# Two of four quarters of a transposed activation go through VectorE and a DRAM scratch instead of TensorE

## The reference

```python
def first_block(x, ...):
    n = rmsnorm(x, attn_norm)
    mix = four_mixers(n @ w_in)                # gated delta net, mLSTM, RG-LRU, RWKV
    x = x + mix @ w_out                        # blocks o0..o3
    n = rmsnorm(x, ffn_norm)                   # operand "x1"
    x = x + (silu(n @ w_gate) * (n @ w_up)) @ w_down   # blocks fg, fu, d
    return rmsnorm(x, final_norm)

def second_block(x, mem, ...):
    h = rms_norm(x, norm_in_g)                 # operand "x2"
    proj = h @ w_in_2                          # first block of it: va0
    ya, yb, ym = moba(...), dilated(...), memory_attention(...)
    merged = sum(sigmoid(gate_i) * (y_i @ w_proj_i))
    return rms_norm(x + merged @ w_out_2, norm_final_g)
```

## Time and profile before

| | |
|---|---|
| time, median of 3 runs | 2382.24 us (2382.02 to 2383.36) |
| time of the profiled execution | 2382.23 us |
| its span in the trace | 2380.4 us |
| PE busy | 2355.0 us, 99% |
| DVE busy | 1489.1 us, 63% |
| ACT busy | 1129.3 us, 47% |
| POOL busy | 257.7 us, 11% |
| DMA queue of SP (q1) | 53.7% of the 16 engines' span |
| DMA queue of GpSimd (q0) | 3.3% |
| mean granted TensorE clock | 0.998 of full speed |

### The profile page before, as it was taken

The page is one execution under the profiler, slowest core; times in us unless marked ns, Lnnn a source line. Parts: engine busy times, 40 slices in busy tenths (PEclk is TensorE's granted clock), DMA queues, the critical chain, the costliest instruction groups (busy, mean ns, idle before and its releaser), DMA issues.

```text
span 2380.4 us, 31332 instructions
## 1 busy us (share of the span) xinstructions
PE 2355.0 (99%) x12768; PEld 1956.3 (82%) x12768; DVE 1489.1 (63%) x1929; ACT 1129.3 (47%) x1423; POOL 257.7 (11%) x383
## 2 busy tenths in 40 slices
PE   9999999999999999999999999999999999999998
PEld 7777789988888888888888888888888888888887
DVE  6887757787755656555565666555556655555555
ACT  6635446564543444444444464445444455344444
POOL 0100011210011111110111142200003200000000
PEclk9999999999999999999999999999999999999999
DMA  9643355645666566655665576655446644555563
GB/s 299 197 142 111 123 175 193 210 165 203 204 202 200 197 198 202 202 192 190 203 203 194 183 241 222 217 172 177 160 153 227 212 142 161 193 195 194 191 233 141
DMA packets 255344, 453.46 MB, mean 190 GB/s; under 512 B 12257, under 2 KB 77409, under 8 KB 252897
## 3 DMA queue, kind: packets, MB, share of 16 engines
q1 hardware_dynamic: 241984, 423.65, 53.7%
q0 software_dynamic: 12640, 27.28, 3.3%
q10 hardware_dynamic: 576, 0.53, 0.1%
HBM read 430.97 MB, written 10.49 MB: 185 GB/s over the span
## 4 chain that ended last, share of the span: by engine, by line
PE 92%; DVE 4%; ACT 1%; issue 1%; DMA 0%; POOL 0%; SPq 0%; ACTq 0%; DVEq 0%; POOLq 0%
PE pp L683 25%; PE pp L685 25%; PE pp L684 25%; PE pp L712 7%; PE pp L713 3%; DVE ringL L2016 1%; PE ps L642 1%; PE ps L1295 1%; PE ps L1309 1%; PE ps L831 0%; DMA raw<-in_w_in 0%; ACT ringH L1383 0%; PE pp L718 0%; PE pp L719 0%; PE pp L720 0%
## 5 line engine op out<-in xcount | busy, mean ns | idle before, releaser
L2016 DVE TENSOR_TENSOR ringL<-raw,ringH 128x1024 fp32r<-128x1024 f32 x779 | 962.5, 1243 | 647.5 <-ACT ringH L1383 645.0
L1383 ACT CAST ringH<-raw 128x1024 fp32r<-128x1024 f32 x779 | 814.8, 1050 | 972.2 <-PE pp L685 864.0
L683 PE MATMUL pp<-ringH,nS 128*128 128x512 f32 x1376 | 543.1, 395 | 0.0
L685 PE MATMUL pp<-ringH,nS 128*128 128x512 f32 x1376 | 536.3, 390 | 0.0
L684 PE MATMUL pp<-ringL,nS 128*128 128x512 f32 x1376 | 535.8, 389 | 0.0
L712 PE MATMUL pp<-nS,ringH 128*128 128x512 f32 x992 | 362.8, 407 | 6.6 <-DVE ringL L2010 2.8
L685 PEld LDWEIGHTS pp<-ringH,nS 128*128 128x128 f32 x1376 | 258.3, 188 | 54.5
L683 PEld LDWEIGHTS pp<-ringH,nS 128*128 128x128 f32 x1376 | 258.4, 188 | 52.9 <-issue 0.4
L684 PEld LDWEIGHTS pp<-ringL,nS 128*128 128x128 f32 x1376 | 258.5, 188 | 51.5 <-issue 0.2
L713 PE MATMUL pp<-nS,ringL 128*128 128x256 f32 x992 | 279.1, 281 | 0.0
L683 PE MATMUL pp<-ringH,xS 128*128 128x512 f32 x704 | 277.8, 395 | 0.0
(11 more groups left out here) (406 smaller groups left out, 2002.0 us busy)
## 6 DMA issues: line engine op xcount, KB each, us to landing
raw<-in_w_in SPq DMA_DIRECT2D x189, 1024.0 KB, 5.1
raw<-in_ffn_w_gate SPq DMA_DIRECT2D x44, 1024.0 KB, 5.4
raw<-in_ffn_w_up SPq DMA_DIRECT2D x44, 1024.0 KB, 5.1
raw<-in_ffn_w_down SPq DMA_DIRECT2D x44, 1024.0 KB, 5.0
raw<-in_w_out SPq DMA_DIRECT2D x32, 1024.0 KB, 5.1
raw<-in_w_mem_kv SPq DMA_DIRECT2D x16, 1024.0 KB, 5.5
AR<-AR POOLq DMA_DIRECT2D x304, 32.0 KB, 4.7
raw<-in_w_proj_a SPq DMA_DIRECT2D x8, 1024.0 KB, 5.1
```

Of the source, the lines that this page charges most:

```text
L683: mm(o, XH[:, ts(j)], WH, first, False)
L685: t_of[0] = mm(o, XL[:, ts(j)], WH, False, last)
L1383: e.copy(ringH[:, h % NSPL, 0:nh * cols], raw[:, u % NRAW, h0 * cols:(h0 + nh) * cols]).then_inc(*hi.tick(h))
L2016: tt2(ringL[:, h % NSPL, o], raw[:, u % NRAW, h0 * cols:(h0 + nh) * cols], ringH[:, h % NSPL, o].bitcast(F32), SUB).then_inc(*lo.tick(h))
```

## The change

The second and third quarter (q = 1, 2) of x1 and x2 are no longer turned by TensorE.

* Behind the drain of `o1.0`, `o2.0`, `d10.1` and `d10.2`, DVE transposes the 32x32 blocks of the quarter into a buffer `across[q]` (two instructions of 128x512).
* GpSimd then runs `hop`: it writes the 512 KB buffer to a scratch in DRAM with one DMA, waits until that has landed, and issues four DMAs of 128 KB that read it back into the same buffer with the blocks crossed.
* ACT and DVE make the high and low parts from that buffer (`landed_split`), waiting on the DMAs' semaphore.
* `fg0` and `va0` take the rows of their weights in the order k = 0 to 3, 12 to 15, 4 to 7, 8 to 11. The stages stand in the order quarter 0, quarter 3, quarter 1 (behind s8 of `fg0` / `va0`), quarter 2 (behind s12). `stat1` and `stat2` come behind them.
* The squares of `XB` for x2 move from the split stage to the drain of the `d10` blocks.

```diff
-    for q in range(4):
-        L.upto(f"o{q}.0")
-        L.step(3)
+    for q in (0, 3):
+        L.upto(f"o{q}.0", 3)
         L.weave(L.stage(f"split1.{q}"), 1)
+    for n, q in enumerate((1, 2)):
+        L.upto("o3.0", 7 + 4 * n)
+        L.run(f"split1.{q}")
...
-    for q in range(4):
-        L.upto(f"d{NG - 1}.{q}")
-        L.step(3)
+    for q in (0, 3):
+        L.upto(f"d{NG - 1}.{q}", 3)
         L.weave(L.stage(f"split2.{q}"), 1)
+    for n, q in enumerate((1, 2)):
+        L.upto(f"d{NG - 1}.3", 7 + 4 * n)
+        L.run(f"split2.{q}")
...
+        def hop(e, name, to, of, apart):
+            d = hold[name]
+            e.dma_start(d.rearrange("p (t n) -> p t n", t=2), of).then_inc(s_out, 16)
+            e.wait_ge(s_out, 16 * (1 + over.index(name)))
+            for j in range(4):
+                piece = d.rearrange("(i p) (t j c) -> j p t i c", i=4, t=2, j=4)[j]
+                for t in (slice(0, 1), slice(1, 2)) if apart else (slice(0, 2),):
+                    e.dma_start(to[32 * j:32 * j + 32, t, :].rearrange("p t (i c) -> p t i c", i=4), piece[:, t]).then_inc(s_over[name], 16)
...
+            turns = (0, 12, 4, 8) if tag in ("fg0", "va0") else None
...
+                k0 = turns[u // 4] if turns else (u + first_k) % nk
...   ACT
+            def landed_split(name, dst, gain, q):
+                def go(L):
+                    for k in range(4 * q, 4 * q + 4):
+                        e.wait_ge(s_over[f"{name}.{q}"], 64)
+                        act(dst[:, k, 0, :]..., in_runs(across[q])[:, :, k % 4, :], ACT.Copy, scale=gain(k))
+                    if name == "x2":
+                        for b in range(2):
+                            e.wait_ge(*pool.at("xg", q, b))
+                            square(XG, q, b, ssg, junk, "x2g")
+                    yield
...   DVE, at the end of drain(B)
+                if q in across:
+                    own(drain_v)
+                    for tt in range(2):
+                        e.transpose(by_quarter(across[q], tt), in_quarters(XB[:, :, 512 * q:512 * q + 512], tt))
...   GpSimd, in unit(i)
+                if s.last and tag in ("o1.0", "o2.0", f"d{NG - 1}.1", f"d{NG - 1}.2"):
+                    e.wait_ge(*drain_v.at("turned", tag, 1))
+                    hop(e, f"x{1 if tag[0] == 'o' else 2}.{q}", across[q], across[q], False)
```

More of the change, by code:

```diff
@@ L419, in program @@
             "fn_v")}
+        over = ["x1.1", "x1.2", "x2.1", "x2.2"]
+        s_out = sem("s_out")
+        s_over = {n: sem(f"s_over_{n}") for n in over}
         hold = {}
@@ L423, in program @@
             hold[nm] = nc.dram_tensor(nm, [128, n], F32).ap()
+        for n in over:
+            hold[n] = nc.dram_tensor("hop_" + n.replace(".", "_"), [128, 1024], F32).ap()
         def alias(name, off, shape):
@@ L1454, in squares @@
                 what = kind[B.tag]
-                x, to, name = (XB, junk, "x1") if what == "o" else (XC, junk3, "x3")
+                x, to, name = (XB, junk, "x1") if what == "o" else (XB, junk, "x2") if what == "d" else (XC, junk3, "x3")
                 for b in range(2):
                     e.wait_ge(*drain_v.at(*(("b0",) if b == 0 else ()), B.tag))
-                    square(x, int(B.tag[1]), b, ss, to, name)
+                    square(x, int(B.tag[-1] if what == "d" else B.tag[1]), b, ss, to, name)
             def high_h(g):
@@ L1503, in unit @@
                         drain(B)
-                    if kind[B.tag] == "q" and B.tag != "q3" or kind[B.tag] == "o" and B.tag[-1] == "0":
+                    if kind[B.tag] == "q" and B.tag != "q3" or kind[B.tag] == "o" and B.tag[-1] == "0" or B.tag.startswith(f"d{NG - 1}."):
                         squares(B)
@@ L1983, in scalar @@
                 "stat1": stat1,
-                **{f"split1.{q}": split1(q) for q in range(4)}, "stat2": stat2, **{f"split2.{q}": split2(q) for q in range(4)},
+                **{f"split1.{q}": split1(q) for q in (0, 3)}, "stat2": stat2, **{f"split2.{q}": split2(q) for q in (0, 3)},
+                **{f"split1.{q}": landed_split("x1", xS, lambda k: pc("ffn_norm", k), q) for q in (1, 2)},
+                **{f"split2.{q}": landed_split("x2", nS, lambda k: gg[:, k:k + 1], q) for q in (1, 2)},
                 "attA": attA, "attM": attM, "attB": attB,
@@ L2064, in drain @@
                             finish(b)
+                q = int(tag[-1]) if tag.startswith(f"d{NG - 1}.") else int(tag[1]) if what == "o" and tag[-1] == "0" else None
+                if q in across:
+                    own(drain_v)
+                    for tt in range(2):
+                        e.transpose(by_quarter(across[q], tt), in_quarters(XB[:, :, 512 * q:512 * q + 512], tt)).then_inc(
+                            *drain_v.tick("turned", tag, tt))
                 if tag in h_crossed:
@@ L2846, in stat2, with landed_split, go @@
                 yield
+            def landed_split(name, dst, gain, q):
+                def go(L):
+                    for k in range(4 * q, 4 * q + 4):
+                        h_, l_ = (dst[:, k, n, :].rearrange("p (a c) -> p a c", c=32) for n in range(2))
+                        e.wait_ge(*sp_a.at(name, k))
+                        stt(out=l_, in0=in_runs(across[q])[:, :, k % 4, :], scalar=gain(k), in1=h_.bitcast(F32), op0=MUL,
+                            op1=SUB).then_inc(*sp_v.tick(name, k))
+                    yield
+                return go
             def scaled_split(name, dst, pname, ks):
@@ L2943, in vector @@
                 **{f"mix{m}": split("mix", nS, lambda k: mix[:, k, :], range(4 * m, 4 * m + 4)) for m in range(4)}, "stat1": stat1,
-                **{f"split1.{q}": scaled_split("x1", xS, "ffn_norm", range(4 * q, 4 * q + 4)) for q in range(4)},
-                "stat2": stat2, **{f"split2.{q}": scaled_split("x2", nS, None, range(4 * q, 4 * q + 4)) for q in range(4)}, "gains": gains,
+                **{f"split1.{q}": scaled_split("x1", xS, "ffn_norm", range(4 * q, 4 * q + 4)) for q in (0, 3)},
+                "stat2": stat2, **{f"split2.{q}": scaled_split("x2", nS, None, range(4 * q, 4 * q + 4)) for q in (0, 3)}, "gains": gains,
+                **{f"split1.{q}": landed_split("x1", xS, lambda k: pc("ffn_norm", k), q) for q in (1, 2)},
+                **{f"split2.{q}": landed_split("x2", nS, lambda k: gg[:, k:k + 1], q) for q in (1, 2)},
                 "attA": attA, "attM": attM, "attB": attB,
@@ L3078, in finals @@
                 e.wait_ge(*st_a.at("x2", 3, 1))
-                e.wait_ge(*pool.at("xg", 3, 1))
+                e.wait_ge(*drain_v.at("turned", f"d{NG - 1}.2", 1))
+                e.wait_ge(*pool.at("xg", 2, 1))
                 for n in range(8):
```

19 lines of the change are left out of this document (11 added, 8 removed).

## The result

The changed kernel takes 2393.44 us (median of 8 runs, 2388.83 to 2399.18), the kernel before 2382.80 (8 runs on the same chip, 2381.92 to 2385.39). The ratio is 1.0045, 95% interval 1.0036 to 1.0054. It was forecast at 2383.1, at most 2389.5. The kernel before by itself has runs near 2382 and runs near 2385 us, these mostly at a mean granted clock of 0.995 or 0.996 instead of 0.997 or 0.998, so a median can jump by 2 us between the two; the ratios set all runs against all and follow the mean more than the median.

The account below looks back on a forecast made before the run. TensorE was taken as the bound, busy 99% of the span. Profiled time 2382.23 - 3.6 (groups) + 0.6 (x1) + 0.3 (x2, k = 8) + 3.6 (x2, GpSimd) = 2383.1 us; 8-in-10 range 2379.2 to 2389.5.

Parts of the forecast that it names:

- The gain of the removed groups: TensorE in x1 and x2: 8 groups of four transposes removed, 0.45 us each, 3.6 us saved, the ceiling.
- Nothing else uses GpSimd here: In x1 GpSimd was taken to have only the two hops, both covered, by 5 and 3 us.
- The short waits for k = 4 and k = 8: TensorE waits 0.3 us where each begins, for splits behind weights: 0.6 us in x1, 0.3 in x2.
- The squares ahead of k = 12: ACT's moved squares might delay k = 12 at s5; nothing booked, with about half a us to spare.
- The hop: GpSimd's write, wait and four issues: 5.7 + 4 x 0.54 = 7.85 us held, data there 4.2 us later.
- slower by GpSimd's queue: Rival: in x2 a hop holds GpSimd over 9.8 us, net loss passes 4.8 us; about 2390 us, 22%.
- XG 3 late, the stall at s9 of `va0`: In x2 GpSimd's product comes behind both hops, delaying ACT, weights and k = 4; TensorE stalls 3.6 us.
- P: Time in x2 until which the second hop holds GpSimd, forecast at 1379.05 us.
- I take 0: VectorE's added transposes could make its `low` late by up to 1.4 us a quarter; booked at nothing.
- 1.3 to 1.8 us each: Duration taken for each of GpSimd's products XG in x2.

Follow-up runs that it names:

- x1_mended: Changed kernel with the first layer's part alone, GpSimd's two constant loads issued early, ACT's squares of the last quarter behind its splits; 2380.58 us, ratio 0.9992.
- x1_only: Changed kernel with the second layer's part undone, so x2 is turned by TensorE as before; 2382.97 us, ratio 1.0001.
- x2_only: Changed kernel with the first layer's part undone, so x1 is turned by TensorE as before; 2391.26 us, ratio 1.0035.
- gains_early: Changed kernel with GpSimd's two constant loads in a stage of their own, issued ahead of the hops; 2392.6 us, ratio 1.0043.
- x2_memset: The second layer's part alone, with GpSimd's products of quarters 1 to 3 replaced by constant fills that read no SBUF; 2384.10 us, ratio 1.0000.
- trains_dma: Kernel before plus unused series of two-input GpSimd products in feed-forward blocks, some directly behind extra GpSimd DMA issues; 2388.34 us, ratio 1.0021.
- x2_apart: The second layer's part alone, with a wait on GpSimd between each two products XG; 2384.55 us, ratio 1.0007.
- both_apart: Changed kernel, both layers, with early constant loads, ACT's last-quarter squares behind its splits, and waits between the products XG; 2384.13 us, ratio 1.0006.
- trains_two: Kernel before plus unused series of GpSimd products with two different inputs in feed-forward blocks, no extra DMA issues; 2383.00 us, ratio 0.9998.
- x2_gap: The second layer's part alone, with one tiny GpSimd fill and a wait between the hop and the series of products; 2386.78 us, ratio 1.0009.
- all_mended: Changed kernel with early constant loads, XG 1 and 2 made during their hop's write, and ACT's last-quarter squares behind its splits; 2385.37 us, ratio 1.0008.
- x2_xg_inside: The second layer's part alone, with GpSimd making XG 1 and 2 while their hop's write is under way; 2386.56 us, ratio 1.0013.
- x1_gains_early: The first layer's part alone, with GpSimd's two constant loads issued ahead of the hops; 2383.18 us, ratio 0.9999.

## Why the prediction was wrong, step by step

- **The gain of the removed groups**, 8 at 0.45 us, 3.6 in all: right. `x1_mended` gives 1.85 for four.
- **"Nothing else uses GpSimd here"** (x1): the step that failed first. The stage `gains` is queued behind the moved stages, and I costed its move at nothing. By the runs this was 2.05 us of stall and the 1.6 at the lower clock. I had followed GpSimd's queue for x2 only. The 2.05 and the 1.6 are the profiled execution's; in `x1_only` it was 1.2 and nothing.
- **The short waits for k = 4 and k = 8**, 0.3 us each: not there. Both stalls at these places had other causes; in `x1_mended` TensorE never stops in x1.
- **The squares ahead of k = 12**, booked at nothing with "about half a us to spare": 1.3 us in x2, and 1.0 in x1, where the squares did not even move but the new order asks for k = 12 eight steps sooner. It was named as a danger, for the moved squares alone, and should have had its term in both layers.
- **The hop**, 7.85 us of GpSimd: 5.6 and 7.8 us in x1, 5.7 and 6.7 in x2. The issues took 0.6 each, as taken. The rival "slower by GpSimd's queue" needed 9.8 us a hop and is refuted; its sign was right for another reason.
- **XG 3 late, the stall at s9 of `va0`**: the mechanism came as described, ACT waiting for GpSimd's product behind the hops and its weights behind that. In the kernel before's time XG 3 began at 1377.6 (1382.28 less 4.7) against P = 1379.05; the stall was 2.3 us instead of 3.6.
- **"I take 0" for VectorE's cover, and the range**: the step that made it wrong in size. I counted when GpSimd's products would be done, not what they do to VectorE. Both read two inputs from SBUF, and the new order puts six of them in one series beside `low`, directly behind DMA issues. x2 as a whole costs 9.73 us in `x2_only`, 6.74 in `gains_early`, -0.55 with no reads, and 1.87 in the changed kernel's own trace, where the two took turns. The earlier trace rows held the sign: one pair of the same products took 3.52 us and another 2.55. I used it as a range of prices, "1.3 to 1.8 us each", and did not ask who was beside the slow one. It was a `low`, 1.88 us long, as VectorE's timeline of the kernel before shows:

```profile
1354.79 1.88 DVE L2016 TENSOR_TENSOR ringL<-raw,ringH 128x1024 fp32r<-128x1024 f32 x1
```

The Trainium skill, "SBUF — State Buffer", "Who interferes with whom", has just this: GpSimd and VectorE share a pair of ports, an exclusive lock, and a VectorE instruction with two inputs in SBUF contends for it with a GpSimd instruction that reads SBUF, not with one that only writes. The turns agree with it (2.3 us for a product or a `low` that waits for the other's 1.2 to 1.3), and so do the fills of `x2_memset`, beside which every `low` took 1.2. The hold over a whole series, in `x2_only` of a `low` that began first, goes beyond it.

What stays open: that the slower runs of the changed kernel (up to 2399.18) are those in which the series holds a `low` fits the 6.7 and 9.7 us of two related kernels and the lower clock, but no trace of such a run is here. What exactly makes a hold is open too. And the feed-forward part, where no instruction differs, took 1.55 us longer in two traces and 0.78 in a third.

## What to carry to other kernels

When a stage is moved in an engine's program, list everything behind it in every queue and price each; loads that were harmless early can meet the weights when late. Two engines that read SBUF together are a resource like a queue: where one instruction has two durations in the trace, look at what runs beside the long one before using it as a range. And where the ceiling is 3.6 us, a single new stall of 2 us with a fall of the clock behind it takes the whole gain.

## What the runs showed of the hardware that I had not expected

- A GpSimd series of 2, 4 or 6 products directly behind its own DMA issues kept VectorE's two-input subtraction out to the end: 3.59, 6.17, 8.53 us instead of 1.23 (`trains_dma`, five of five). With waits between the products the longest was 2.29 in `x2_apart` and 2.78 in `both_apart`. One series behind its issues took turns, in the changed kernel.
- Without an issue ahead (`trains_two`), the two alternate instruction by instruction, 1.3 us becoming 2.3 for GpSimd and 1.2 becoming 2.1 for VectorE, and TensorE behind a ring of four halves didn't notice.
- A memset of GpSimd in the same place, 0.5 us each, disturbed nothing (`x2_memset`).
- After a stall of TensorE of 2 to 3 us the granted clock fell to 1.2 GHz for some us (pitch 0.43 instead of 0.23) in the changed kernel's x1, `x2_apart`, `x2_gap` and `all_mended`, but not in the changed kernel's x2 (2.3) nor in `x2_xg_inside` (2.4); after one of 9 us, in `x2_only`, it was at 1.2 GHz while idle and for 5 us of work.
- Behind some stalls the feed-forward part ran a little slower at full granted clock: 66.35 us instead of 66.26 from one `fg` drain to the next in the changed kernel, `x1_only`, `x1_gains_early` and the later part of `trains_dma`, and in the first two kernels 66.70 and 66.76 for the first two. It came in no trace without a stall in or ahead of that part. The cause is open.
